# 16-bit floats for the two crossed products of the query, U and V tiles

## What is computed

```
h = rms_norm(x, norm_ffn_g[l]) * (1.0 + sc2) + sh2
q = (xt @ w_query).reshape(T, N_RET_HEADS, 2, HALF_KEY)      # 16 query tiles of 128 columns
s = einsum('thpd,hpnd->thpn', q, sub_keys)                    # top 16 of each half, then top 16 of the sums
a = gelu(einsum('chkd,cd->chk', u_tab[idc], xc))              # u_tab: 16384 x 1024
coef = gates * a
y = einsum('chk,chkd->cd', coef, v_tab[idc])                  # v_tab: 16384 x 1024
x = x + g2 * y
```

## Time and profile before

| what | value |
|---|---|
| median of three runs | 3501.65 us (3500.31 to 3506.22) |
| span of the profiled execution | 3507.9 us |
| PE busy | 97% of the span |
| PEld busy | 89% |
| DVE busy | 85% |
| ACT busy | 44% |
| POOL busy | 33% |
| mean granted TensorE clock | 0.989 |
| HBM, mean | 245 GB/s; 330 to 355 GB/s from the groups on |

### The profile page before, as it was taken

One profiled execution on the slowest core, in us unless ns is written; L12 is line 12 of the kernel. 1 busy time (PEld: TensorE's weight loads), 2 busy tenths in 40 slices (PEclk: granted clock), 3 DMA queues, 4 the chain that ended last, 5 costly groups with the idle time before them and its releaser, 6 DMA issues.

```text
span 3507.9 us, 61155 instructions
## 1 busy us (share of the span) xinstructions
PE 3394.8 (97%) x19278; PEld 3136.9 (89%) x19278; DVE 2964.6 (85%) x6035; ACT 1559.4 (44%) x2317; POOL 1165.8 (33%) x1070
## 2 busy tenths in 40 slices
PE   6999999999999999999999999999999999999999
PEld 5767778999999999999977677789999999999999
DVE  6899777998888788888869997789988887888888
ACT  3574424345555433333346734433455553333333
POOL 0000003116555555464400000041265564555443
PEclk9999999999999999999999999999999999999999
DMA  5312263569999999999923123536699999999998
GB/s 198 103 61 72 90 258 103 166 194 331 354 349 329 329 345 346 350 342 349 331 89 93 56 83 117 218 110 184 222 340 350 355 334 333 356 351 337 353 347 283
DMA packets 421662, 868.83 MB, mean 248 GB/s; under 512 B 167824, under 2 KB 233360, under 8 KB 421008
## 3 DMA queue, kind: packets, MB, share of 16 engines
q1 hardware_dynamic: 310512, 544.87, 46.9%
q0 software_dynamic: 73728, 268.47, 21.5%
q10 hardware_dynamic: 37152, 52.45, 4.0%
HBM read 774.41 MB, written 85.98 MB: 245 GB/s over the span
## 4 chain that ended last, share of the span: by engine, by line
PE 45%; issue 25%; DVE 13%; POOL 10%; DMA 2%; ACT 2%; POOLq 0%; DVEq 0%; SPq 0%; ACTq 0%
PE ps L857 9%; PE ps L859 9%; PE ps L858 9%; POOL gbuf L563 5%; PE ps L613 5%; POOL spare L577 5%; PE ps L615 5%; PE ps L614 5%; DVE yT L1405 3%; DVE i L1647 2%; DVE v L1643 1%; DMA raw<-stream 1%; DVE S_ring L1653 1%; DMA gbuf<-u_rows,ids_u 1%; PE ps L626 1%
## 5 line engine op out<-in xcount | busy, mean ns | idle before, releaser
L921 ACT CAST w_hi<-raw 128x1024 fp32r<-128x1024 f32 x680 | 715.5, 1055 | 866.4 <-DMA raw<-stream 831.5
L613 PE MATMUL ps<-h_hi,w_hi 128*128 128x384 f32 (+1 forms) x2944 | 1058.6, 360 | 16.5 <-DVE w_lo L1611 14.0
L615 PE MATMUL ps<-h_hi,w_lo 128*128 128x384 f32 (+1 forms) x2944 | 1035.9, 352 | 0.0
L614 PE MATMUL ps<-h_lo,w_hi 128*128 128x384 f32 (+1 forms) x2944 | 1035.4, 352 | 0.0
L857 PE MATMUL ps<-cf_hi,w_hi 128*128 128x384 f32 x2048 | 691.5, 338 | 8.8 <-DVE cf_lo L1823 4.8
L859 PE MATMUL ps<-cf_hi,w_lo 128*128 128x384 f32 x2048 | 689.7, 337 | 0.0
L858 PE MATMUL ps<-cf_lo,w_hi 128*128 128x384 f32 x2048 | 689.4, 337 | 0.0
L577 POOL TENSOR_TENSOR spare<-spare 128x1 f32<-128x1 f32 x504 | 359.0, 712 | 990.8 <-DVE a_sp L1635 508.9
L613 PEld LDWEIGHTS ps<-h_hi,w_hi 128*128 128x128 f32 x2944 | 554.3, 188 | 69.8 <-DVE w_lo L1611 19.8
L615 PEld LDWEIGHTS ps<-h_hi,w_lo 128*128 128x128 f32 x2944 | 553.7, 188 | 36.8
L614 PEld LDWEIGHTS ps<-h_lo,w_hi 128*128 128x128 f32 x2944 | 554.7, 188 | 34.9 <-issue 2.4
(11 more groups left out here) (257 smaller groups left out, 4139.1 us busy)
## 6 DMA issues: line engine op xcount, KB each, us to landing
raw<-stream SPq DMA_DIRECT2D x682, 512.0 KB, 5.5
gelu_scratch<-g_out ACTq DMA_DIRECT2D x256, 192.0 KB
cg<-gelu_scratch SPq DMA_DIRECT2D x256, 192.0 KB, 6.1
c_scratch<-stage SPq DMA_DIRECT2D x128, 256.0 KB
cg<-c_scratch SPq DMA_DIRECT2D x256, 128.0 KB, 5.1
qT<-ada SPq DMA_DIRECT2D x32, 512.0 KB, 6.2
cgate<-ada SPq DMA_DIRECT2D x32, 512.0 KB, 5.5
w_rows<-ada SPq DMA_DIRECT2D x32, 512.0 KB, 7.0
```

The lines of the kernel that those rows point to most:

```text
L613: nc.tensor.matmul(ps[:, b, 0:n], wh, hi[:, c, t0:T], start=c == 0, stop=False)
L614: nc.tensor.matmul(ps[:, b, 0:n], wh, lo[:, c, t0:T], start=False, stop=False)
L615: mm = nc.tensor.matmul(ps[:, b, 0:n], wl, hi[:, c, t0:T], start=False, stop=c == C - 1)
L921: nc.scalar.copy(w_hi[:, s], raw[:, s]).then_inc(hi_done, 1)
```

## The change

For the query, U and V tiles the two crossed products become 16-bit. The weight is scaled by 256 when it is rounded, the activation and the coefficient carry a scale of 16 and its inverse, so that remainders don't underflow. A tile now has `w_hi` (fp32r, scaled), and in place of `w_lo` a pair `w16[s]` over the same bytes as `raw[s]`: half 0 the remainder in 16 bits, half 1 a 16-bit copy of `w_hi`. The first is written by DVE with one fused instruction or by POOL with two; the second by ACT in a new instruction, `half_word`, which waits for the remainder (it overwrites the raw tile). `h16` and `cf16` hold the same pair for activations and coefficients. The copy in 16 bits of `h_hi` is made by POOL, that of `cf_hi` by ACT. PE does the 8 high by high products first, then waits for `w16_done`, then does the 16 products in 16 bits. All other tiles stay as they were.

```diff
 # GpSimd
+                def low16(s, i):
+                    high = pool.snap(l * NT + i + 1)
+                    up = pool.snap(l * (C * 2 + U_POOL) + i - I_QRY + 1)
                     pool.wait_ge(hi_done, high)
-                    nc.gpsimd.tensor_tensor(w_lo[:, s], raw[:, s], w_hi[:, s].bitcast(F32),
+                    nc.gpsimd.tensor_tensor(raw[:, s], raw[:, s], con[:, K_UP:K_UP + 1].rearrange("p (o q) -> p o q", o=1)
+                                            .broadcast_to([P, C, P]), ALU.mult).then_inc(raw_up, 1)
+                    pool.wait_ge(raw_up, up)
+                    nc.gpsimd.tensor_tensor(w16[:, s, 0], raw[:, s], w_hi[:, s].bitcast(F32),
                                             ALU.subtract).then_inc(lo_done, 1)
...
+                low16(0, I_QRY)
+                low16(1, I_QRY + 1)
+                for c in range(C):
+                    pool.wait_ge(hhi_done, (2 * l + 1) * C + c + 1)
+                    nc.gpsimd.tensor_tensor(h16[:, c, 1], h_hi[:, c].bitcast(F32), con[:, K_ONE:K_ONE + 1].broadcast_to([P, T]),
+                                            ALU.mult).then_inc(h16_done, 1)
 # TensorE
+                def product16(s, g, e, k, t0=0):
+                    b, n = s % 2, T - t0
+                    pe.wait_ge(bank_read[b], e)
+                    pe.wait_ge(hi_done, g + 1)
+                    for c in range(C):
+                        nc.tensor.matmul(ps[:, b, 0:n], w_hi[:, s, c], h_hi[:, c, t0:T], start=c == 0, stop=False)
+                    pe.wait_ge(w16_done, k)
+                    for c in range(C):
+                        nc.tensor.matmul(ps[:, b, 0:n], w16[:, s, 0, c], h16[:, c, 1, t0:T], start=False, stop=False)
+                        mm = nc.tensor.matmul(ps[:, b, 0:n], w16[:, s, 1, c], h16[:, c, 0, t0:T], start=False, stop=c == C - 1)
+                    mm.then_inc(tile_done, 1)
...
-                def experts(s, j, g, first, last):
+                def experts(s, j, g, k, first):
                     pe.wait_ge(cf_ready, j + 5)
-                    pe.wait_ge(lo_done, g + 5)
+                    pe.wait_ge(hi_done, g + 1)
...
+                    pe.wait_ge(w16_done, k)
 # ScalarE
+                def half_word(s, g):
+                    act.wait_ge(lo_done, g + 5)
+                    nc.scalar.mul(w16[:, s, 1], w_hi[:, s].bitcast(F32), X_DOWN).then_inc(w16_done, 1)
...
+                half_word_at(I_QRY)
                 updated_square(C - 1)
+                half_word_at(I_QRY + 1)
...
                 for i in range(I_QRY, I_U):
                     high_at(i + 2)
+                    if i > I_QRY:
+                        half_word_at(i + 1)
...
                 def u_tile(u):
+                    half_word_at(I_U + u + 1)
                     high_at(I_U + u + 2)
...
-                    nc.scalar.copy(cf_hi[s][:], coef[:, s % 2]).then_inc(cf_hid, 1)
+                    nc.scalar.mul(cf16[s][:, 1], coef[:, s % 2], X_DOWN)
+                    nc.scalar.mul(cf_hi[s][:], coef[:, s % 2], X_DOWN).then_inc(cf_hid, 1)
...
                     for s in range(4):
                         coef_high((s + 1) % 4, r + (s + 1) // 4)
+                        half_word((s + 1) % 4, l * NT + I_W + 4 * r + s + 1)
                         high_in((s + 2) % 4, I_W + s + 2, r)
 # VectorE (the same form in u_low and weight_low; cf16 and h16 alike)
-                    nc.vector.tensor_tensor(w_lo[:, u % 4], raw[:, u % 4], w_hi[:, u % 4].bitcast(F32),
-                                            ALU.subtract).then_inc(lo_done, 1)
+                    nc.vector.scalar_tensor_tensor(out=w16[:, u % 4, 0], in0=raw[:, u % 4], scalar=W_UP,
+                                                   in1=w_hi[:, u % 4].bitcast(F32), op0=ALU.mult,
+                                                   op1=ALU.subtract).then_inc(lo_done, 1)
```

More of the change, by code:

```diff
@@ L632, in first_pair, with split_done, first_queries, query @@
                                 mm.then_inc(tile_done, 1)
+                def split_done(i):
+                    return l * (NT - I_QRY) + i - I_QRY + 1
+                def product16(s, g, e, k, t0=0):
[9 more added lines that the diff above has]
+                    mm.then_inc(tile_done, 1)
+                def first_queries():
+                    i = I_QRY
+                    for q in range(2):
+                        pe.wait_ge(bank_read[q], l * (NE // 2) + i // 2 + 1)
+                    pe.wait_ge(hi_done, l * NT + i + 2)
+                    for c in range(C):
+                        pe.wait_ge(hhi_done, (2 * l + 1) * C + c + 1)
+                        for q in range(2):
+                            nc.tensor.matmul(ps[:, q], w_hi[:, q, c], h_hi[:, c], start=c == 0, stop=False)
+                        if c == 0:
+                            pe.wait_ge(w16_done, split_done(i + 1))
+                        pe.wait_ge(h_ready, (2 * l + 1) * C + c + 1)
+                        for q in range(2):
+                            nc.tensor.matmul(ps[:, q], w16[:, q, 1, c], h16[:, c, 0], start=False, stop=False)
+                        pe.wait_ge(h16_done, l * C + c + 1)
+                        for q in range(2):
+                            mm = nc.tensor.matmul(ps[:, q], w16[:, q, 0, c], h16[:, c, 1], start=False, stop=c == C - 1)
+                            if c == C - 1:
+                                mm.then_inc(tile_done, 1)
+                def query(i):
+                    product16(i % 4, l * NT + i, l * (NE // 2) + i // 2 + 1, split_done(i))
                 def proj(i, hi, lo, chunks=None):
@@ L849, in _ @@
                 W_ORDER = tuple(range(2, C)) + (0, 1)
-                def experts(s, j, g, first, last):
+                def experts(s, j, g, k, first):
                     pe.wait_ge(cf_ready, j + 5)
-                    pe.wait_ge(lo_done, g + 5)
-                    for c in range(C) if last else W_ORDER:
+                    pe.wait_ge(hi_done, g + 1)
+                    for c in W_ORDER:
                         if first and c < 2:
@@ L857, in experts, with last_experts @@
                         nc.tensor.matmul(ps[:, c, P:T], w_hi[:, s, c], cf_hi[s][:], start=first, stop=False)
[L858 to L867, removed]
+                    pe.wait_ge(w16_done, k)
+                    for c in W_ORDER:
+                        nc.tensor.matmul(ps[:, c, P:T], w16[:, s, 0, c], cf16[s][:, 1], start=False, stop=False)
+                        mm = nc.tensor.matmul(ps[:, c, P:T], w16[:, s, 1, c], cf16[s][:, 0], start=False, stop=False)
+                    mm.then_inc(tile_done, 1)
+                def last_experts(s, j, g, k):
+                    pe.wait_ge(cf_ready, j + 5)
+                    pe.wait_ge(w16_done, k)
+                    for c in range(C):
+                        nc.tensor.matmul(ps[:, c, P:T], w_hi[:, s, c], cf_hi[s][:], start=False, stop=False)
+                        nc.tensor.matmul(ps[:, c, P:T], w16[:, s, 0, c], cf16[s][:, 1], start=False, stop=False)
+                        mm = nc.tensor.matmul(ps[:, c, P:T], w16[:, s, 1, c], cf16[s][:, 0], start=False, stop=True)
+                        if c == C - 1:
+                            mm.then_inc(tile_done, 1)
+                        if c == 0:
+                            pe.wait_ge(row_used, (l + 1) * 2 * P + 4)
+                        nc.tensor.transpose(ps[:, c, 0:P], y_sp[:, c * P:(c + 1) * P], ident).then_inc(y_tr, 1)
                 pe.wait_ge(h_ev, 2 * l + 2)
```

108 lines of the change are left out of this document (68 added, 40 removed).

## The result

The changed kernel takes 3706.4 us (median, 3699.43 to 3709.69) against 3503.73 us (3500.31 to 3506.22) of the kernel before in the same runs: a ratio of 1.057, with a 95% interval from 1.0551 to 1.0589. It is slower by 203 us. The execution that was profiled took 3699.43 us, with a span of 3697.6 us, 189.7 us more than the span of before. It is the fastest of its four.

What follows compares the result with a forecast made beforehand. PE was taken to bound the kernel before, DVE and an ACT-DVE loop the changed one. 130 + 50 + 8 + 8 - 3 = 193 us on the span of 3507.9 gives 3701, less 6.3: 3695 us, range 3610 to 3785.

Steps and rivals of the forecast that it cites:

- What bounds the kernel: Kernel before: PE sets V's pace at 4.16 us a tile, with transfers nearly as full (DMA share 0.99).
- PE's part: Query, U and V tiles: 164.6 ns per 16-bit matmul, net 0.09 us saved a tile, 49 us if PE binds everywhere.
- V tiles, +130: V stage: a new loop between ACT and DVE sets the pace, +65 us a layer, +130 in all.
- the ring: V: half_word waits for DVE's remainder, DVE for ACT's coefficients queued behind half_word; one turn per tile, 4.71 us.
- the turn: V: one pass around the ACT and DVE loop, one tile, summed to 4.71 us against PE's 4.07.
- The groups, +50: Groups: DVE sets the pace, losing 2.18 us in each pair of remainders; +25 us a layer, +50 in all.
- Case 3: V's loop holds, but in the groups DVE's slack absorbs the rest: 3645 us, chance 22%.
- Small parts, V's start and PE's gain, +13 together: Query start and routing +8 us, Gelu's delay where V begins +8, PE's gain in last U tiles and queries -3.
- The delay of Gelu that was put at V's start: Where V begins: Gelu of the last U tile stands behind half_word, what follows comes 4 us later; +8 us.
- Cases 1 and 2: V's turn shorter than forecast: PE binds again, 3453 us (6%), or V and groups keep their times, about 3500 (4%).
- case 4: V's loop plus late transfers: tiles landing 0.3 us late on average cost 77 us; 3770 us, chance 14%.
- case 5: PE's gaps lower the granted clock for a part of V, 150 us: 3850 us, chance 4%.

Runs made afterwards that it cites:

- norow_b: The kernel before, with 252 of the 256 V gathers of the two layers replaced by a copy of a few KB: 3501.4 us, ratio 0.9991.
- u_act: The changed kernel, with ACT making high_at(u + 2) ahead of half_word_at(u + 1) in a U tile's step: 3640.6 us, ratio 1.0375.
- all3: The changed kernel with DVE's V remainders and ACT's U-tile copies reordered, POOL's first remainders and ACT's first half_words later at the normalisation: 3476.8 us, ratio 0.9913.
- v_dve: The changed kernel, with DVE making weight_low(k + 1) ahead of mixed_low(k + 1) in V: 3549.1 us, ratio 1.0119.
- half_v: v_dve with each gathered V row, all but four, fetched for 64 of the 128 tokens only: 3655.7 us, ratio 1.0422.

## Why the prediction was right

3695 us was forecast, 3706.4 measured; on the spans, 3701 against 3697.6. Most of the 11 us lies in the step from span to median: the prediction took off 6.3 us, as in the profile of before, while here the profiled execution is the fastest and its span lies 8.8 us below the median. By its steps:

- **What bounds the kernel.** Right: V ran at PE's 4.16 us a tile, and norow_b shows that the full DMA share beside it cost next to nothing (V 2 us shorter without the gathers).
- **PE's part.** Forecast: 164.6 ns for a 16-bit matmul, tile 4.07 us. Measured: 162.2 ns and 4.01 us. The 4.6 ns over the columns at 128 columns did not carry over to 384, where it is 2.2. The rule that the prediction cites from the Trainium skill ("TensorE: Matmul & The Clock Gate", Back-to-back issue gap), 162.5 ns, was the better one here, though the Trainium skill gives it for a single matmul by itself. No time hung on it, since PE doesn't bind in the changed kernel.
- **V tiles, +130.** Measured +128.4, and the ring is the one described, wait by wait. But the turn was put at 4.71 us and is 4.59: the two surcharges of 0.06 for fused instructions were wrong. Fused remainders take 1218 to 1220 ns, as the plain one did (1220); the 1281 of `weigh` was not a price of fusion. What the sum lacked makes up for it: the pauses of DVE at the turns of its loop (5.09 us in the chain above), which had been covered before, cost 4.4 and 4.5 us in layer 1, and the first and the last tile 7.2 together (8.2 + 8.2 less two turns). 128 x 0.12 = 15.4 us too much against 16.1 us left out. So the total is right by compensation, which is luck; the mechanism is right on its own merits. Among the measured parts, ACT's 16-bit copy has a pitch of 0.97 us (forecast 0.95).
- **The groups, +50.** Measured +43.7. The 37 waits of 2.1 us each are there (78.6 us in layer 1 against 28 waits and 48.1 us before), and the waits for gathered rows fell from 14.2 to 5.9 (forecast: to 7). Case 3, that the groups absorb it all, is out.
- **Small parts, V's start and PE's gain, +13 together.** Measured +17.6 for the rest of the span, but not from the places named. Ahead of the groups 19.4 us were lost (first `one_j` at 776.0 and 784.8 in layer 1), where 8 were forecast. The landmarks of layer 1 divide them, in us:

| stretch, layer 1 | before | after | forecast |
|---|---|---|---|
| first of the four additions to the first query matmul | 17.4 | 21.1 | +1 |
| query tiles | 107.0 | 104.5 | -3 in both layers, with the last U tiles |
| first U tile to the first `one_j` (routing) | 142.4 | 149.2 | +3 |

The normalisation lost 3.7 us: the prediction looked at whether POOL keeps up, not at what POOL's two instructions do to DVE beside them. Routing lost 6.8, over twice what was forecast; u_act takes 3.1 of them back, so about half comes from the same order of `half_word` and `w_hi` as in the groups. PE's gain in the query tiles, 2.5 us a layer, is real. The delay of Gelu that was put at V's start is real too (`half_word` waits 3.03 us at 1254.88 and Gelu starts at 1256.80), but it lies after V's first matmul, so it is part of the V stage's 603.5; the stretch between the last `one_j` and V got 4.4 us shorter in layer 1 and stayed in layer 2 (52.5). The step that failed inside the right total is the size of the terms ahead of the groups and the place of the one at V's start.
- **The other cases.** Cases 1 and 2 need a turn near PE's tile; it is 4.59 us. Against case 4, no late landings (ACT's waits for raw tiles vanished in V); against case 5, no lower clock (0.99 and 1.00 in the windows). The low end of the range was added up wrongly: its terms, 74 + 28 + 0, give 102 and not 108. Nothing hangs on that.

What remains open: why DVE pauses at the turn of its loop, and what the half of routing's loss is that u_act does not take back.

## What to carry to other kernels

What a new instruction costs here is set by what stands behind it in its queue and what its wait ties together, far more than by its length: with the same 544 copies of 1.06 us the kernel takes 220 us more in one order of the queues than in another (3706.4 against 3486.4 us). Before adding a wait between two engines that already wait for each other, write down the ring and add up one turn; if it is longer than the bound engine's step, look for two instructions on one of the engines whose exchange opens the ring. A pause that was hidden by a lead (here of DVE at its loop turns) becomes visible once the lead is gone, so look for it in the profile of before, at every turn: here it showed at three of six.

## What the runs showed of the hardware that I had not expected

**POOL slows DVE's two-input instructions.** POOL in the changed kernel, beside the four additions of 10.02 us above:

```profile
509.67 1.89 POOL L559 TENSOR_TENSOR raw<-raw,con 128x1024 f32<-128x1024 f32 x1
511.64 2.74 POOL L562 TENSOR_TENSOR w<-raw,w_hi 128x1024 f16<-128x1024 f32 x1
514.34 2.34 POOL L559 TENSOR_TENSOR raw<-raw,con 128x1024 f32<-128x1024 f32 x1
516.76 2.73 POOL L562 TENSOR_TENSOR w<-raw,w_hi 128x1024 f16<-128x1024 f32 x1
```

An addition of 0.69 us takes 2.5 us while POOL works, about as long as one instruction of POOL, four beside four (2.09, 2.79, 2.27 and 2.78 us; each ends about 0.5 us after one of POOL). In the kernel before POOL has two instructions there, and two of the four additions are long (2.70 and 2.78 us). With POOL held back (all3) the four take 2.86 us. The Trainium skill ("SBUF — State Buffer", SBUF: two separate sides) says that VectorE and GpSimd share a pair of ports as an exclusive lock, which a VectorE instruction with two SBUF inputs takes for its whole length against a GpSimd instruction that reads SBUF; the trace agrees.

**Transfers to half the partitions.** Gathers into 64 partitions brought the whole traffic from 352 to 257 GB/s at a full DMA share, and lengthened V by 55 and 57 us (v_dve to half_v). The Trainium skill ("SBUF — State Buffer", Door 1: The DMA port swizzle) says that partitions 0 to 63 reach only 8 of the 16 ports, with 196 GB/s against 328 measured for a transfer of 1 MiB by itself. The runs agree in direction; whether the ports or the DMA engines behind them were uneven here no view shows.

**Weight loads.** In the records a 16-bit weight load takes 98 ns, a 32-bit one 189. PE's pace per matmul fell by only 11 ns (173.3 to 162.2). In the query tiles, with 512 columns (213.3 ns), 32-bit matmuls come every 227 ns and 16-bit ones every 216: the same 11 ns, and the 32-bit ones are again some 13 ns above their columns, although a load of 188 ns has more room there. That speaks against the load as what the 32-bit pace waited for. No run changes the load alone, so it is not shown, and it holds for these widths: at 128 columns the 32-bit matmuls of the kernel before come every 109 to 112 ns, the 16-bit ones every 58.
